# Expert stage with 80 token places an expert instead of 88

## What is computed

```python
def moe_swiglu(h, w_router, w_gate, w_up, w_down):       # D = 1024, 8 experts of width 3584
    logits = (h @ w_router).astype(jnp.float32)
    top_val, top_idx = lax.top_k(logits, TOP_K)            # TOP_K = 2
    top_w = jax.nn.softmax(top_val, axis=-1)
    gates = jnp.sum(jax.nn.one_hot(top_idx, N_EXPERTS, dtype=jnp.float32) * top_w[..., None], axis=-2)
    out = jnp.zeros_like(h)
    for e in range(N_EXPERTS):
        y = swiglu(h, w_gate[e], w_up[e], w_down[e])       # (silu(h @ w_gate) * (h @ w_up)) @ w_down
        out = out + gates[..., e:e + 1].astype(h.dtype) * y
    return out
```

## Time and profile before

| | us |
|---|---|
| median of the three timed runs | 2958.57 |
| lowest and highest | 2953.74, 2962.55 |
| span of the profiled execution | 2960.3 |
| PE busy in it | 2790.1 |
| expert stage in it, first to last record of L1471 and L1480 | 655.3 to 1570.7 |

### The profile page before, as it was taken

The page is one execution under the profiler, slowest core; times in us unless marked ns, Lnnn a source line. Parts: engine busy times, 40 slices in busy tenths (PEclk is TensorE's granted clock), DMA queues, the critical chain, the costliest instruction groups (busy, mean ns, idle before and its releaser), DMA issues. The chain is left out here.

```text
span 2960.3 us, 70140 instructions
## 1 busy us (share of the span) xinstructions
PE 2790.1 (94%) x31522; PEld 2063.3 (70%) x31522; DVE 579.2 (20%) x1423; ACT 357.7 (12%) x896; POOL 86.3 (3%) x130
## 2 busy tenths in 40 slices
PE   6889999989999999999998898989999999898999
PEld 3758857669899999999997545865444444545883
DVE  0120001121000000000001323652222201232331
ACT  1010001011000000000001211221111100121110
POOL 0000000000000000000000001210000000000000
PEclk9999999989999999999998899999999999999999
DMA  8664435629999999999993011001222221302432
GB/s 344 259 248 147 149 129 228 234 107 354 353 388 408 381 383 410 373 379 399 385 399 158 29 71 44 3 2 57 85 71 79 78 75 64 132 29 71 157 142 85
DMA packets 80391, 583.94 MB, mean 197 GB/s; under 512 B 8912, under 2 KB 8912, under 8 KB 10064
## 3 DMA queue, kind: packets, MB, share of 16 engines
q1 hardware_dynamic: 79920, 580.15, 50.3%
q10 hardware_dynamic: 288, 1.05, 0.1%
HBM read 580.11 MB, written 1.05 MB: 196 GB/s over the span
## 5 line engine op out<-in xcount | busy, mean ns | idle before, releaser
L1471 PE MATMUL ps<-arena,ring 128*64 128x88 f32 x14336 | 552.6, 239 | 23.1 <-issue 19.8
L1471 PEld LDWEIGHTS ps<-arena,ring 128*64 128x64 f32 x14336 | 546.9, 137 | 27.9 <-issue 25.6
L2830 PE MATMUL ps<-hT,ring 128*128 128x256 f32 (+2 forms) x1472 | 455.3, 472 | 5.6 <-ACT hT L472 3.4
L2830 PEld LDWEIGHTS ps<-hT,ring 128*128 128x128 f32 x1472 | 274.5, 190 | 185.2 <-issue 166.3
L359 PE MATMUL ps<-ring,arena 128*128 128x512 f32 x896 | 390.6, 597 | 5.0 <-DVE arena L2735 3.8
L359 PEld LDWEIGHTS ps<-ring,arena 128*128 128x128 f32 x896 | 171.0, 192 | 218.5 <-issue 212.2
L1480 PE MATMUL ps<-arena,ring 128*64 128x88 f32 x7168 | 275.9, 239 | 6.1 <-issue 5.8
L1480 PEld LDWEIGHTS ps<-arena,ring 128*64 128x64 f32 x7168 | 273.1, 137 | 7.6 <-issue 7.3
L1621 DVE TENSOR_TENSOR arena<-arena,ps 128x88 f32<-128x88 f32 x224 | 55.1, 246 | 511.7 <-ACT arena L1600 511.7
L981 PE MATMUL ps<-hT,ring 128*128 128x256 f32 (+1 forms) x736 | 152.7, 370 | 2.6 <-ACT hT L470 2.6
L1600 ACT ACTIVATE arena<-ps 128x88 f32<-128x88 f32 x224 | 54.5, 243 | 814.0 <-PE ps L1471 814.0
(11 more groups left out here) (469 smaller groups left out, 2161.8 us busy)
## 6 DMA issues: line engine op xcount, KB each, us to landing
ring<-in_stream SPq DMA_DIRECT2D x547, 1024.0 KB, 7.2
par<-in_params SPq DMA_DIRECT2D x1, 3397.0 KB, 28.8
h<-in_x ACTq DMA_DIRECT2D x2, 512.0 KB, 8.3
cx<-in_ctx SPq DMA_DIRECT2D x2, 512.0 KB, 30.2
out<-h SPq DMA_DIRECT2D x4, 256.0 KB, 2.0
par<-in_params SPq DMA_DIRECT2D x1, 941.0 KB, 6.5
```

Of the source, the lines that this page charges most:

```text
L1471: last = nc.tensor.matmul(ps[m:m + 64, up_bank[j], half * P:half * P + CAP], w[:, k, half * P + m:half * P + m + 64], hTe[:, k, :], start= ...
L2830: last = nc.tensor.matmul(ps[:, 2 * BANKS_CONV[f % RING] + half, tok], w[:, k, half * P:half * P + P], hT[:, k, tok], start=(k == 0), stop ...
```

## The change

One constant. `CAP` sets the width of the moving operands of L1425, L1471 and L1480, the widths of `hid`, `sg`, `hTe` and `yT`, the evictions' widths, the rows used by the transposes and by the spread, the `slots` row, and the threshold of the flag. The list of instructions has the same rows on every engine, with 80 in place of 88 in their shapes (and 160 and 320 for 176 and 352); SyncE's list is the same.

```diff
-CAP = 88
+CAP = 80
```

## The result

The changed kernel has a median of 2925.95 us (2923.5 to 2927.82), the kernel before, beside it, 2958.32. The ratio is 0.9882, 95% interval 0.9869 to 0.9896: by that ratio some 35 us less, of which the interval leaves 31 to 39 (the two medians alone lie 32 apart). Forecast were 2903.5 us and a range from 2885 to 2922. The direction was right, the size was not, and the time lies above the range.

A forecast was written before the change was run, and what follows sets the result against it. PE was taken to bound the expert stage, the DMA close behind: 51 us from seven experts plus 4 from expert 0 made 55 off 2960.3, 2905.3; timed runs lie 1.7 lower, so 2903.5 us, range 2885 to 2922.

The forecast's parts named there:

- What bounds the kernel: Expert stage: PE leads narrowly at 2.425 us a tile, against 2.485 for the DMA; its waits name issue, never a DMA.
- Part 1, matmuls: L1471 and L1480: a tile takes 2.213 us, 0.212 less, saving 71 us over 336 tiles; the gather at L1425 saves 1.6.
- The low end of 57 from the 64-column records: Expert-stage matmuls: a straight line from 30 ns at 64 columns to 37.9 at 88 would save only 57 us.
- the rival of a floor by weight loads: Expert-stage matmuls: weight loads keep each record at 37.9 ns, so nothing is gained, 2958 us; chance 0.03.
- Part 2, evictions: ScalarE and VectorE, each tile: eight columns fewer save at most 0.02 us, hidden under PE; GpSimd's copies bring nothing.
- Part 3, instruction fetch: PE's instruction fetches, expert stage: expert 0 saves 4 of 8.9 us; the looped experts lose 1.0 us each.
- at most 14 of 42 tiles, 3.0 us: Looped experts: only the first pass through each loop meets the fetch, so at most 3.0 us an expert is lost.
- Part 4, the DMA as the mate: Experts 1 to 6: PE's 105.7 us meets the DMA's 104.9, late in up; 106.5 an expert, saving 7.3 each.
- the rival of a poorer DMA: Expert-stage weight loads: under full load only 404 GB/s, so 38 us saved, 2921 us; chance 0.20.
- The charge of 0.8 us an expert for coupling: Looped experts: PE and DMA, nearly equal and coupled by seven tile buffers, take 106.5 us, 0.8 above PE's own 105.7.
- The general path: If an expert exceeds 80 tokens, all 336 tiles are loaded and multiplied again with 256 tokens: about 5220 us; chance 0.03.
- The rest of the sum: After the expert stage: work moves with it; loads queued behind the last expert's cost nothing, or 7 us if uncovered.

The follow-up runs named there:

- quarter-load pair: The changed kernel (80 places) and the kernel before (88 places), each loading only the first 512 of 2048 columns of every expert-stage weight tile: 2856.97 and 2932.05 us.

## Why the prediction missed

**What bounds the kernel** was read rightly as PE with the DMA close behind, and the count of instructions is indeed unchanged, 70140. The reading stopped too early at the words "never a DMA": in the earlier trace rows PE's waits named issue, and in the earlier trace rows the fetch's pace stood open at 6.1 us against batches of 5.07.

**Part 1, matmuls: right.** 2.213 us a tile was forecast, ticks of 2.21 are measured, and the quarter-load pair gives 75 us for 71 + 1.6. The low end of 57 from the 64-column records, and the rival of a floor by weight loads, are out; at 72 places the records are 31.25 ns apart in the median tile, still on the line (31.25).

**Part 2, evictions: right**, hidden as forecast.

**Part 3, instruction fetch: the step that failed.** The mechanism was named, and its term of the sum was mis-sized: 12 us charged, 38 measured. In expert 0 a saving of 4 of 8.9 us was expected and about 1 came; in the looped experts 1.0 us each was put down as lost, 7 in all, and the table of stretches shows 9.1 - 5.2 = 3.9 each for six of them and 5.8 for the last. Altogether 12 us were charged where 33 of pauses and 5 of lower clock, 38, were measured. The argument that should have been made needs no new row: if a fetch takes 6.1 us, a block of two tiles loses all of its 0.43 us saving, and a block whose fetch was just covered starts to pause. That is what the counts say: 33 pauses of 1.0 us became 49 of 1.4. The bound "at most 14 of 42 tiles, 3.0 us" was too small as well, against 3.9 measured. It left out the turn's code, which is fetched too, and it took a paced tile to lose at most the 0.212 us that it would have saved, when some pauses grew by more: before the change the DMA's share in experts 1 to 6 was 0.96 to 0.97, after it 0.99 to 1.01. That the rest left to the DMA is what shortened some fetches before was not tested by itself. The lower clock behind the longest pauses was listed among what could go wrong, without a price.

The Trainium skill bears on this at two points. "Runtime: NRT & Kernel Launch", section "Instruction fetch mechanics", gives the refill as blocks of 16 KiB, 256 instructions; the trace agrees, with a pause every 127 or 128 pairs of a load and a matmul. The same section calls the cost of such a boundary mostly hidden, and says that kernels prefer full unrolling; here the measurement decides otherwise, with 55 us of issue waits in the changed stage and 16 us for one expert written out, and it agrees where the DMA is a third busy (1.6 us of issue waits) or PE slower (4.4 us with 96 places).

**Part 4, the DMA as the mate: right in where, wrong in how.** The DMA did go to a share of 1.00 and 406 GB/s, in the last expert 418, above the 404 that the rival of a poorer DMA took for its limit (expert 0, at 0.91 and 343, and expert 1, at 0.99 and 393, stayed below), and landings took 8.8 us (median). But PE never waited for a tile: by the landings each tile was there 1.5 us or more before its first matmul. What came late was not the tiles but the instructions fetched between them. The charge of 0.8 us an expert for coupling had no counterpart. That rival's number, 2921, lies nearest to the measurement, for a reason that the trace refutes.

**The general path** did not run: the packets are as many as before, 80391.

**The rest of the sum** held: what follows the stage moved with it, and the backlog cost nothing that can be seen.

## What to carry over

When an engine is paced by several suppliers that run at almost the same rate, list them all before pricing a speed-up: here tiles at 2.485 us, and 16 KB of instructions every 6.1 us for each two tiles. A wait marked "issue" that recurs after a fixed number of instructions is a supplier too, and it shares the DMA engines with the data. If such pauses show already, take the time of a block from the slower of its two sides; code size is then worth time too: a loop in place of one written-out copy of 14 tiles brought 6 to 11 us here, where 9% fewer columns in 336 tiles brought 35.

## What the hardware showed that was not expected

A tile loaded to 64 partitions instead of 128 kept the DMA engines almost as busy as the whole one, 0.96 at 207 GB/s with 636 ns for a packet of 8 KB instead of 309, while a quarter of the columns on all partitions brought the share down to 0.36. The time of an instruction fetch depended on the weight traffic beside it: with 80 places 6.3 us (median from one to the next) beside full loads, 5.5 beside half the partitions, and at most 4.8 beside a quarter of the columns, where PE itself sets the pace. It did not depend on the tiles queued (6.2 with five instead of seven). Whether the busy share or the length of the packets beside it matters, and where in the fetch the added time is spent, no run here tells. After a pause of 2.46 us the granted clock was 0.50 for 3.4 us, though PE worked right up to the pause and from its end on; of two pauses about as long, one of 2.11 us ahead of 1229.17 was followed by such a stretch and one of 2.15 us ahead of 907.29 was not.
